# A decoder block pair on one core: unused products in TensorE's pauses, two later places for the inverse's steps, and an output tail in two halves

## What is computed

```python
x = layernorm(ALPHA * x + rwkv7_mixer(x) , ln_g[0], ln_b[0])      # "wout", then ln 0
x = layernorm(ALPHA * x + diff_mixer(x, k_sh, v_sh), ln_g[1], ln_b[1])  # "bout", then ln 1
m = sigmoid(gate_a) * (pool @ w_pool_out) + sigmoid(gate_b) * (conv @ w_conv_out)  # "pc"
h = h + rms_norm(m @ w_o, g_post_mix)                             # "wo"
u = rms_norm(h, g_pre_mlp)
f = square(relu(u @ w_up)) @ w_down                               # "up", "down", in two halves of 4096
return h + rms_norm(f, g_post_mlp)                                # the tail
```

## Time and profile before

| | |
|---|---|
| median of 3 runs | 2483.46 us |
| lowest and highest | 2481.92 and 2485.06 us |
| the profiled execution's own time | 2486.26 us |
| its span, first to last instruction | 2484.5 us |
| mean granted TensorE clock | 0.984 |
| PE busy | 2398.0 us (97%) |
| DVE busy | 1518.5 us (61%) |
| ACT busy | 1188.1 us (48%) |
| mean DMA rate | 170 GB/s |

### The profile page before, as it was taken

One profiled execution on the slowest core, in us unless ns is written; L12 is line 12 of the kernel. 1 busy time (PEld: TensorE's weight loads), 2 busy tenths in 40 slices (PEclk: granted clock), 3 DMA queues, 4 the chain that ended last, 5 costly groups with the idle time before them and its releaser, 6 DMA issues.

```text
span 2484.5 us, 49504 instructions
## 1 busy us (share of the span) xinstructions
PE 2398.0 (97%) x20577; PEld 2283.8 (92%) x20577; DVE 1518.5 (61%) x1841; ACT 1188.1 (48%) x1501; POOL 15.5 (1%) x31
## 2 busy tenths in 40 slices
PE   8999999988999999999899999999999999999997
PEld 7999998878999899999899998999999888999886
DVE  7577576557664455656789895554954444555444
ACT  5576453224454456654653345356544433444342
POOL 0000000000000000000000000000000000000000
PEclk9999999998999999999999999999999999999999
DMA  8355565314555654465456564555566556666654
GB/s 275 119 178 171 172 196 160 115 52 151 170 164 186 187 168 153 153 189 176 140 173 182 164 186 144 187 161 179 168 199 176 187 187 186 186 185 185 186 186 135
DMA packets 217221, 423.50 MB, mean 170 GB/s; under 512 B 17088, under 2 KB 19472, under 8 KB 216320
## 3 DMA queue, kind: packets, MB, share of 16 engines
q1 hardware_dynamic: 207232, 397.46, 52.3%
q0 software_dynamic: 2656, 12.17, 1.6%
q10 hardware_dynamic: 7152, 11.25, 1.5%
HBM read 412.43 MB, written 8.39 MB: 169 GB/s over the span
## 4 chain that ended last, share of the span: by engine, by line
PE 88%; DVE 7%; ACT 3%; issue 2%; DMA 0%; ACTq 0%; DVEq 0%; SPq 0%
PE ps L483 27%; PE ps L484 26%; PE ps L485 26%; PE ps L694 3%; DVE wlo L354 2%; ACT whi L350 1%; PE ps L613 1%; PE ps L599 1%; PE ps L702 1%; DVE regions L1819 0%; DVE act_lo L2015 0%; PE ps L897 0%; ACT regions L1417 0%; ACT L1417 0%; DVE regions L2042 0%
## 5 line engine op out<-in xcount | busy, mean ns | idle before, releaser
L354 DVE TENSOR_TENSOR wlo<-wraw,whi 128x1024 fp32r<-128x1024 f32 x752 | 918.0, 1224 | 866.0 <-ACT whi L350 864.9
L483 PE MATMUL ps<-act_hi,whi 128*128 128x256 f32 (+1 forms) x4736 | 1358.7, 287 | 39.4 <-DVE act_lo L2126 12.7
L484 PE MATMUL ps<-act_lo,whi 128*128 128x256 f32 (+1 forms) x4736 | 1341.3, 283 | 0.0
L485 PE MATMUL ps<-act_hi,wlo 128*128 128x256 f32 (+1 forms) x4736 | 1339.7, 283 | 0.0
L350 ACT ACTIVATE whi<-wraw 128x1024 fp32r<-128x1024 f32 x752 | 794.1, 1059 | 1109.4 <-PE ps L485 1093.4
L483 PEld LDWEIGHTS ps<-act_hi,whi 128*128 128x128 f32 x4736 | 900.5, 190 | 45.7 <-issue 30.8
L484 PEld LDWEIGHTS ps<-act_lo,whi 128*128 128x128 f32 x4736 | 903.5, 191 | 1.1
L485 PEld LDWEIGHTS ps<-act_hi,wlo 128*128 128x128 f32 x4736 | 900.1, 190 | 0.0
L485 PE MATMUL ps<-whi,regions_r 128*128 128x512 f32 x512 | 203.0, 396 | 0.0
L484 PE MATMUL ps<-wlo,regions_r 128*128 128x512 f32 x512 | 203.0, 396 | 0.0
L483 PE MATMUL ps<-whi,regions_r 128*128 128x512 f32 x512 | 203.0, 396 | 0.0
(11 more groups left out here) (323 smaller groups left out, 1416.4 us busy)
## 6 DMA issues: line engine op xcount, KB each, us to landing
wraw<-in_a_w_in SPq DMA_DIRECT2D x128, 512.0 KB, 4.2
wraw<-in_w_up SPq DMA_DIRECT2D x128, 512.0 KB, 3.9
wraw<-in_w_down SPq DMA_DIRECT2D x128, 512.0 KB, 4.3
wraw<-in_w_in SPq DMA_DIRECT2D x112, 512.0 KB, 3.8
wraw<-in_b_w_qg SPq DMA_DIRECT2D x64, 512.0 KB, 3.8
wraw<-in_a_w_out SPq DMA_DIRECT2D x32, 512.0 KB, 3.7
wraw<-in_w_k_shared SPq DMA_DIRECT2D x32, 512.0 KB, 4.4
wraw<-in_w_v_shared SPq DMA_DIRECT2D x32, 512.0 KB, 4.3
```

Of the source, the lines that this page charges most:

```text
L354: nc.vector.tensor_tensor(wlo[:, q % RING], wraw[:, q % RING], whi[:, q % RING].bitcast(F32), ALU.subtract).then_inc(lo_ready, 1)
L483: mm(o, hi_s, hi_m, start=first, stop=False, skip_group_check=True)
L484: mm(o, hi_s, lo_m, start=False, stop=False, skip_group_check=True)
L485: i = mm(o, lo_s, hi_m, start=False, stop=last, skip_group_check=True)
```

## The change

`keep_warm(n, b)` issues n products of a 128x128 matrix of ones and the 128x128 identity, both fp32, into bank b; nobody reads them. They stand in the nine pauses: 28 at the start (on a tile of ones that VectorE writes first, as the constants are not loaded yet), 22 before `turn_y` and 15 after it, 4 before and 7 after each of `spread(0)` and `spread(1)`, 15 before "bout", 22 before "pc", 15 before "wo", 3 before and 7 after `spread(2)`. "scatter" moves from half slab 31 to 33, the y and z steps from half slabs 35 to 62 to half slabs 38 to 62, and `first_turn(0, ...)` one slab later on VectorE. The last group of "down1" takes slabs 0 to 3 as before, then slabs 4 to 7 for the first 128 tokens, then slabs 4 to 7 for the other 128; the loop around the groups of "down1" is written out for its second round. The tail runs once for each half of the tokens, and the stores go out by halves. A semaphore of its own for the last gain row is replaced by a count on `extra_loaded`.

```diff
+        warm = gate[:, 0:P]
-        steps_at[31] = [("scatter", 0, 0, 0)]
+        steps_at[33] = [("scatter", 0, 0, 0)]
-            steps_at[35 + 7 * n_ // 8] += [(kind, c, f, lv)]
+            steps_at[38 + 25 * n_ // 32] += [(kind, c, f, lv)]
...
-            for c in range(0, 4, 2):
-                store_out(sp, c)
+            for tb, c in ((0, 0), (0, 1), (0, 2), (0, 3), (1, 0), (1, 2)):
+                store_out(sp, tb, c)
...
+            def wm_last(G, outs, xh, xl, k0):
+                at = [(q, kk, tb) for q in range(RING) for kk in range(2) for tb in range(2)]
+                at += [(q, kk, tb) for tb in range(2) for q in range(RING, SLABS) for kk in range(2)]
+                for q, kk, tb in at:
+                    if kk == tb == 0:
+                        pe.wait_ge(lo_ready, SLABS * G + q + 1)
+                    done, k = q == SLABS - 1 and kk == 1, k0 + 2 * q + kk
+                    three(outs[tb], ..., first=False, last=done,
+                          sig=slab_used if kk == 1 and tb == 1 else S["tile_mm"] if done else None)
+            def keep_warm(n, b, lhs=cs("ones"), rhs=cs("ident")):
+                for _ in range(n):
+                    mm(ps[:, b, 0:P], lhs, rhs, start=True, stop=True)
...
+            pe.wait_ge(S["warm_ready"], 1)
+            keep_warm(28, 7, warm, warm)
...
+            keep_warm(22, 0)
             for j2 in range(4):
                 turn_y(j2)
+            keep_warm(15, 0)
...
             last_group(G0["wout"] + 3, ahi, alo, mean_of(0), token_sums(0, True))
+            keep_warm(4, 1)
             spread(0, ("scale", "shift"))
+            keep_warm(7, 1)
...
+                if s == 0:
+                    keep_warm(15, 0)
                 ws_group(G0["bout"] + s, ...)
...
                     pe.wait_ge(acc_act, ACC_ACT["gates"] + 7)
+                    keep_warm(22, 0)
                     pe.wait_ge(S["cstd"], 1)
...
             last_group(G0["wo"] + 3, ahi, alo, None, token_sums(2, False))
+            keep_warm(3, 1)
             spread(2, ("scale",))
+            keep_warm(7, 1)
...
+                with pe.Fori(0, 1 if half else 2) as i:
+                    for s in range(2):
+                        down_pair(i, s, range(2))
+                if half:
+                    down_pair(1, 0, range(2))
+                    down_pair(1, 1, range(1))
+                    wm_last(G0[down] + 7, [bank(2), bank(3)], fhi, flo, KT)
...
+            for tb in range(2):
+                act.wait_ge(S["acc_dve"], ACC_DVE["down1"] + 4 + tb)
+                st.do(a(junk[:, 0:GW], yS[:, tb, 3 * GW:4 * GW], ACT.Square, accum_out=ssr[:, tb, 3:4]), sig["ssq"])
+                act.wait_ge(S["ssum"], tb + 1)
+                st.do(a(rstd_[:, tb:tb + 1], rsm[:, tb:tb + 1], ACT.Sqrt, bias=eps6), sig["sstd"])
...
+            st.do(nc.vector.memset(warm, 1.0), sig["warm_ready"])
...
-                    if (s, u) == (2, 0):
+                    if (s, u) == (2, 1):
                         for f in range(2):
                             first_turn(0, f)
...
+            for tb in range(2):
+                if tb:
+                    dve.wait_ge(slab_used, SLABS * GROUPS)
+                else:
+                    dve.wait_ge(S["tile_mm"], 10)
+                st.do(tt(yS[:, tb, last], yS[:, tb, last], bank(2 + tb), ALU.add), sig["acc_dve"])
+                st.do(tt(yG[3][:, tb, :], yS[:, tb, last], grow[:, last], ALU.mult))
...
+                for c in range(4):
+                    st.do(stt(Htok[:, tb, cols], yG[c][:, tb, :], rrstd[:, one_tb], Htok[:, tb, cols], ALU.mult, ALU.add), sig["out_cols"])
```

More of the change, by code:

```diff
@@ L364, in group_slabs, with store_out @@
                     hook(u)
-        def store_out(eng, c):
+        def store_out(eng, tb, c):
             cols = slice(c * GW, (c + 1) * GW)
-            for tb in range(2):
-                eng.wait_ge(S["out_cols"], 2 * c + tb + 1)
-                eng.dma_start(out.rearrange("o (b p) n -> p (o b) n", p=P)[:, tb, cols], Htok[:, tb, cols]).then_inc(S["out_stored"], 16)
+            eng.wait_ge(S["out_cols"], 4 * tb + c + 1)
+            eng.dma_start(out.rearrange("o (b p) n -> p (o b) n", p=P)[:, tb, cols], Htok[:, tb, cols]).then_inc(S["out_stored"], 16)
         @block.sync
@@ L522, in wm_group @@
                         hook(q)
+            def wm_last(G, outs, xh, xl, k0):
[5 more added lines that the diff above has]
+                    done, k = q == SLABS - 1 and kk == 1, k0 + 2 * q + kk
+                    three(outs[tb], xh[:, k, tb * P:(tb + 1) * P], xl[:, k, tb * P:(tb + 1) * P], whi[:, q % RING, kk], wlo[:, q % RING, kk],
+                          first=False, last=done, sig=slab_used if kk == 1 and tb == 1 else S["tile_mm"] if done else None)
             def packed(b0):
@@ L1057, in _, with down_pair @@
                 pe.wait_ge(acc_act, ACC_ACT[up] + 7)
-                with pe.Fori(0, 2) as i:
-                    for s in range(2):
+                def down_pair(i, s, parts):
                         if s:
@@ L1062, in _ @@
                         pe.wait_ge(acc_dve, 2 * i + (ACC_DVE[down] + s - 1))
-                        for part in range(2):
+                        for part in parts:
                             wm_group(4 * i + (G0[down] + 2 * s + part), [bank(2 * s), bank(2 * s + 1)], fhi, flo, first=part == 0, last=part == 1,
                                      x_ready=lambda k: 8 * half + k // 4 + 1, k0=KT * part, ready=S["f_ready"])
+                with pe.Fori(0, 1 if half else 2) as i:
[5 more added lines that the diff above has]
+                    wm_last(G0[down] + 7, [bank(2), bank(3)], fhi, flo, KT)
         @block.scalar
@@ L1460, in squares @@
                         st.do(a(junk[:, 0:GW], yS[:, tb, c * GW:(c + 1) * GW], ACT.Square, accum_out=ssr[:, tb, c:c + 1]),
-                              sig["ysq"] if c < 3 and tb else sig["ssq"] if tb else None)
+                              sig["ysq"] if tb else None)
             def wide_evac(dst, p, fn, last):
@@ L2327, in _ @@
                         group_slabs(dve, split_lo, G, gained(s - 1) if half and s and part else None)
+                    if half and s == 3:
+                        break
                     dve.wait_ge(slab_used, SLABS * (G + 1))
@@ L2334, in _ @@
             last = slice(3 * GW, 4 * GW)
-            st.prev()
-            st.do(tt(yG[3], yS[:, :, last], grow[:, last].unsqueeze(1).broadcast_to([P, 2, GW]), ALU.mult))
-            dve.wait_ge(S["ssq"], 1)
-            st.do(nc.vector.tensor_reduce(rsm, ssr, AX.X, ALU.add))
-            st.prev()
-            st.do(tt(rsm, rsm, q4sq, ALU.mult), sig["ssum"])
-            dve.wait_ge(S["sstd"], 1)
-            st.do(nc.vector.reciprocal(rrstd, rstd_))
-            st.prev()
-            st.do(tt(rrstd, rrstd, q4, ALU.mult))
-            st.prev()
-            for c in range(4):
-                cols = slice(c * GW, (c + 1) * GW)
-                for tb in range(2):
-                    st.do(stt(Htok[:, tb, cols], yG[c][:, tb, :], rrstd[:, tb:tb + 1], Htok[:, tb, cols], ALU.mult, ALU.add), sig["out_cols"])
+            for tb in range(2):
+                one_tb = slice(tb, tb + 1)
+                if tb:
[3 more added lines that the diff above has]
+                st.do(tt(yS[:, tb, last], yS[:, tb, last], bank(2 + tb), ALU.add), sig["acc_dve"])
+                st.prev()
+                st.do(tt(yG[3][:, tb, :], yS[:, tb, last], grow[:, last], ALU.mult))
+                dve.wait_ge(S["ssq"], tb + 1)
+                st.do(nc.vector.tensor_reduce(rsm[:, one_tb], ssr[:, tb, :], AX.X, ALU.add))
+                st.prev()
+                st.do(tt(rsm[:, one_tb], rsm[:, one_tb], q4sq[:, one_tb], ALU.mult), sig["ssum"])
+                dve.wait_ge(S["sstd"], tb + 1)
+                st.do(nc.vector.reciprocal(rrstd[:, one_tb], rstd_[:, one_tb]))
+                st.prev()
+                st.do(tt(rrstd[:, one_tb], rrstd[:, one_tb], q4[:, one_tb], ALU.mult))
+                st.prev()
+                for c in range(4):
+                    cols = slice(c * GW, (c + 1) * GW)
+                    st.do(stt(Htok[:, tb, cols], yG[c][:, tb, :], rrstd[:, one_tb], Htok[:, tb, cols], ALU.mult, ALU.add), sig["out_cols"])
 WEIGHTS = ["a_w_in", "a_w1", "a_a1", "a_w2", "a_a2", "a_w_out", "w_k_shared", "w_v_shared", "b_w_qg", "b_w_out", "b_lambda", "ln_g",
```

16 lines of the change are left out of this document (8 added, 8 removed).

## The result

The changed kernel takes **2459.95 us** (median of 4 runs, 2458.18 to 2460.45), against 2483.78 for the kernel before in the same rounds (4 runs, 2481.92 to 2485.06): a ratio of 0.9907, 95% interval 0.9891 to 0.9922, or 23.8 us less. The forecast was 2458.9. The profiled execution took 2460.14 us with a span of 2458.3, 26.2 less than the profiled span of before; that one lay 2.5 above its median of these rounds and this one 0.2 above its own, which explains the difference between 26.2 and 23.8.

A forecast was written before the change was run, and what follows sets the result against it. TensorE was taken as the bound, busy 2398.0 of 2484.5 us, with cold stretches costing time only where it sets the pace. Terms summed to 24.6 us off the 2483.46 median, forecasting 2458.9, range 2454 to 2466.

The forecast's parts named there:

- Start: Before the first product: fillers let slab 0 run warm, gaining 1.7 us, bounds +2.0 and -1.8.
- Inverse: In group "g": moved steps remove both waits and the cold stretches behind them, gaining 8.4 us, bounds 2 and 9.
- packed steps repay part: Rival in the inverse: packed steps meet VectorE mid-split and repay 3 of 8.4 us, giving 2464; chance 0.13.
- "wout", "bout", "pc", "wo": First products of these groups run warm instead of cold, gaining 2.6, 2.2, 1.7 and 2.7 us.
- Spreads 0 and 1: Warm spread products end earlier, so VectorE starts earlier: 0.8 us and 0.6 us gained.
- the prediction's own sign of being wrong: Half-clock stretches remaining behind the pauses, longer pauses, or waits between y and z steps would refute the prediction.
- Tail: After TensorE's last product: work by token halves ends 5.3 us after it instead of 9.3, gaining 3.9 us.
- transposes: Rival at "wout": transposes don't count as activity, so the clock stays down there, giving 2461.5; chance 0.05.
- overlong fillers: Slower rival at the pauses: all fillers cost 0.43 us and outlast them, giving 2493; chance 0.02.
- fillers that don't hold the clock: Rival at the pauses: clock falls stay, only inverse and tail gains are left, giving 2471; chance 0.06.
- half of the cold time: Rival for the cold stretches: each gives back half its length, 29.0 us instead of 10.6, giving 2440.5; chance 0.02.
- New waits bring new falls: Rival: warm TensorE after the spreads waits near 2 us and the clock falls again, giving 2463 to 2465; chance 0.13.

The follow-up runs named there:

- e6: Changed kernel with twice the fillers before "bout" (30), "pc" (44) and "wo" (30): 2470.09 us, ratio 0.9949 to the kernel before.
- e8: e7 plus eight fillers in the 2.17 us wait ahead of the recurrence: 2460.4 us, ratio 0.9911 to the kernel before.
- e4: Changed kernel with two fp32 128x128 transposes in place of each filler product, except at the start: 2460.77 us, ratio 0.9909 to the kernel before.
- e9: Changed kernel with the token sums before the spreads made 128 columns wide instead of one: 2459.65 us, ratio 0.9904 to the kernel before.
- e5: Changed kernel with scatter still at half slab 33 but y and z steps back at their old half slabs: 2467.79 us, ratio 0.994.
- e7: Changed kernel with three more fillers ahead of the waits between one-column token sums before spreads 0 and 1: 2462.33 us, ratio 0.9919.
- e1: Kernel before with only the inverse's steps moved (scatter, y and z steps, first_turn): 2475.63 us, ratio 0.9973.
- e2: Kernel before with only the last down group in two halves and the tail and stores by halves: 2479.62 us, ratio 0.9983.
- e3: Changed kernel without any filler product, inverse scheduling and tail kept: 2469.25 us, ratio 0.9938 to the kernel before.
- e10: e9 with 32 fillers at the start instead of 28: 2458.92 us, ratio 0.9902 to the kernel before.

## Why the prediction was right, point by point

- **A filler's price** (0.22 us warm, hidden by the pause): right. 44 records in 5.07 us, and e6 paid 9.9 of 10.5 expected. The way to it was not: two records as far apart as in the groups (0.1185) would be 0.24, and by that 22 fillers would just have filled a pause of 5.2. The value came out lower than its own reasoning, and true.
- **Start** (1.7): measured 1.75, with some luck, as it is no fixed gain. With 0.86 to 1.79 us left between fillers and first product (after, e8, e6, e4, e9) slab 0 ran warm; with 1.85 and 1.97 (e5, e7) the clock fell at 12.06 and 12.55 and the gain was 0.1 and -0.3. The same 28 fillers ended between 9.38 and 10.39, since the clock rises at another moment in each execution. The kernels without fillers (e1, e2, e3) are also 0.4 to 1.0 us behind the profiled execution of before here. I had priced only the loss of fillers that run too late, not of those that end too early.
- **Inverse** (8.4): 9.79, and e1 gives 9.8 alone. Both waits went, as worked out; scatter started at 394.21, the lead of the start included. Against the profiled execution of before the term was 1.4 too small. Some 0.5 of it I can name: three fewer half slabs alternate with steps, and a half slab between steps takes 1.60 us where one without takes 1.42. The rest, about 0.9, stays unresolved. It is not more than chance moves this stage: against e2's "g" the same move gains 7.8, and e1's median fell by 7.4, both less than forecast. The rival "packed steps repay part" did not come: the first y step runs its 64 records in 2.08 us with no wait behind the splits.
- **"wout", "bout", "pc", "wo"** (2.6, 2.2, 1.7, 2.7): 2.59, 2.25, 1.67 and 2.75. Counting cold products and multiplying by 0.093 us holds where the pieces come ahead of need. One reserve: of "bout", 0.7 us also came in e1 and e3 without any filler there, since their clock fell for 3.4 us where it was 6.8 before, so a cold stretch's length differs from one execution to the next.
- **Spreads 0 and 1** (0.8 and 0.6): **the step that failed**. Both gave nothing, because the clock fell just as the spread began. By the prediction's own sign of being wrong (half clock behind the pauses) it fails for these two of the nine. I had taken the fillers ahead of the spread to be enough, as in the other pauses, and had not asked about the one-column sums ahead of them. Filling their pauses did not help in e7, making the sums wide did (e9, e10), and then the two terms appear with 0.7 and 0.5, near their forecast size. In the six kernels with fillers and one-column sums the clock fell at 11 of 12 such spreads (one trace each; not at spread 1 in e8), in the two with wide sums at none of four.
- **Waits behind L2057**: they grew where the forecast reasoned it, behind a warmer TensorE, from 4.9 us to 9.3 for the pieces after the first; only the sum over L2057 hides it.
- **Spread 2** (0): 0.02. That its cold products would return nothing is right: the clock no longer falls there, and the waits for VectorE (1.26 and 1.60 us) take up what TensorE gains.
- **Tail** (3.9): 4.43. VectorE's part came as worked out, 9.3 to 5.4 us after TensorE's end (5.3 forecast). The 0.5 left is the last store, which I took to land as late as before: it ends the span 2.7 us after the last operation, and 3.2 before.
- **The rest.** No wait at the loop's turn or at the shared semaphore; 0 was right. The 1.05 of the recurrence was in no step: with the step to "wout" its time varies from kernel to kernel (89.6 to 94.8 us); e1, e2 and e3, without filler, take 93.1, 94.3 and 94.3, and no run separates the fillers' part from chance.

So the total stood for mostly the right reasons: 2458.9 against 2459.95 (the same sum against the profiled span: 24.6 of 26.2). That it lies this close is luck in part: start, inverse, recurrence and tail gave 3.0 more than forecast and the spreads 1.6 less, and the start and the inverse move by 1 to 2 us with the execution that is profiled. Of the rivals, transposes (e4), overlong fillers (e6), repaid inverse (e1), fillers that don't hold the clock (e3) and half of the cold time (e3) are out. "New waits bring new falls" came by half: the waits came (9.3 us against 4.9, none longer than 1.65), and no fall followed one of them. Of the stretches in the changed kernel, one lies in the recurrence, where before had one too, and two at the spreads, where before was cold as well and for longer.

## What to carry to other kernels

Fill a pause of TensorE with unused products only where TensorE sets the pace behind it, and count them from the pause and their price (here 0.224 us for fp32 128x128) so that a few tenths are left: too many are paid one for one, and with none the clock fell at every one of these pauses. Where VectorE sets the pace, a cold TensorE costs little or nothing; 47.6 us of half clock were worth 7 to 10. One trace is one execution: before blaming a code change for a fall, or crediting it with one less, look for the same stretch of code in another kernel's trace. A wait that stands in a fixed order goes by putting independent work ahead of it, and all steps that hang on it have to move along: scatter alone brought a third of the gain.

## What the runs showed of the hardware

- With one-column fp32 products, back to back between fillers, TensorE is busy by the trace (4.20 of 4.20 us in e7), and yet the clock fell behind them, at 11 of 12 spreads; with the same sums 128 columns wide it fell at none of four (e9 and e10), at hardly more time: 4 records take 0.61 us instead of 0.58. The width is the only thing that this edit changes on TensorE; why it matters is not shown, and spread 1 of e8 shows that narrow sums don't bring a fall every time.
- fp32 transposes hold a full clock as well as ordinary products (e4, over 10.5 us with nothing else on TensorE).
- The length of a pause near 2 us does not say whether the clock falls. The same pause of 2.17 us ahead of the recurrence was met by a fall in before, after, e1, e5, e6 and e7 and by none in e2, e3, e4, e9 and e10. At the start 1.85 us had one (e5) and 1.79 had none (e9), with the same filler before both; ahead of L755 1.61 (e6) and 1.67 us (e9) had one.
- The clock falls at other places in executions of nearly the same code (481 in one, 542 in the next, 359, 513 and 544 in a third), for 3.4 or 6.8 us. Inside the recurrence such a fall costs nothing that shows: from the end of "g" to the first slab of "wout" e9, with two, and e10, with none, both take 90.4 us (one pair of traces). Inside "g", where TensorE sets the pace, one of 3.4 us costs 1.3 (e9 at 359.83).
